# First layer's stick-breaking attention: the order of its steps, item by item, and one activation table set for Exp and Ln

## What is computed

```python
z = jnp.einsum('bqhd,bkhd->bhqk', q_blk, k).astype(jnp.float32) * scale
mask = key_pos[None, :] < q_pos[:, None]
log_1mb = jnp.where(mask, jax.nn.log_sigmoid(-z), 0.0)
after = lax.cumsum(log_1mb, axis=3, reverse=True) - log_1mb
w = jnp.where(mask, jnp.exp(jax.nn.log_sigmoid(z) + after), 0.0)
return jnp.einsum('bhqk,bkhd->bqhd', w.astype(v.dtype), v)
```

## Time and profile before

| | |
|---|---|
| median of 3 runs | 4190.07 us (4188.62 to 4195.27) |
| the profiled execution, its own time | 4190.46 us |
| its span, first to last instruction | 4188.7 us |
| TensorE clock granted, mean over the span | 0.917 of full |
| TensorE busy, share of the span (page) | 89% |
| the stretch of `Stick`, first sum matmul to last `XL` | 466.4 to 657.7 us |

### The profile page before, as it was taken

The page is one execution under the profiler, slowest core; times in us unless marked ns, Lnnn a source line. Parts: engine busy times, 40 slices in busy tenths (PEclk is TensorE's granted clock), DMA queues, the critical chain, the costliest instruction groups (busy, mean ns, idle before and its releaser), DMA issues. The chain is left out here.

```text
span 4188.7 us, 48251 instructions
## 1 busy us (share of the span) xinstructions
PE 3738.1 (89%) x18866; PEld 3037.5 (73%) x18866; DVE 2024.5 (48%) x3934; ACT 1698.1 (41%) x3132; POOL 108.0 (3%) x120
## 2 busy tenths in 40 slices
PE   6999678989995898999797999999879999998799
PEld 5888436768883777778675777777767687887686
DVE  3144323364334566676435355555545456555542
ACT  3222463264332333333225344444432555555430
POOL 0011120000000000000000000000000000000000
PEclk9999889989996787778899999999989999999799
DMA  3333303112222112111311111010122211110221
GB/s 124 116 129 105 126 0 121 36 56 96 102 77 75 43 44 61 41 41 44 154 51 41 40 30 30 27 31 26 34 103 76 71 36 36 36 36 16 85 101 41
DMA packets 219706, 265.62 MB, mean 63 GB/s; under 512 B 62684, under 2 KB 142676, under 8 KB 218456
## 3 DMA queue, kind: packets, MB, share of 16 engines
q1 hardware_dynamic: 219480, 262.53, 19.2%
HBM read 191.95 MB, written 70.52 MB: 63 GB/s over the span
## 5 line engine op out<-in xcount | busy, mean ns | idle before, releaser
L320 PE MATMUL bank<-wh,XH 128*128 128x512 f32 x1344 | 554.4, 412 | 40.8 <-DVE wl L304 21.1
L320 PE MATMUL bank<-wh,XL 128*128 128x512 f32 x1344 | 529.4, 394 | 0.0
L320 PE MATMUL bank<-wl,XH 128*128 128x512 f32 x1344 | 529.4, 394 | 0.0
L2394 PE MATMUL bank<-XH,wh 128*128 128x512 f32 x1040 | 428.5, 412 | 32.0 <-DVE wl L2383 19.7
L2394 PE MATMUL bank<-XH,wl 128*128 128x512 f32 x1040 | 412.9, 397 | 0.0
L2394 PE MATMUL bank<-XL,wh 128*128 128x512 f32 x1040 | 411.8, 396 | 0.0
L320 PEld LDWEIGHTS bank<-wh,XH 128*128 128x128 f32 x1344 | 256.3, 191 | 104.3 <-issue 39.2
L320 PEld LDWEIGHTS bank<-wh,XL 128*128 128x128 f32 x1344 | 256.5, 191 | 60.0 <-issue 10.0
L320 PEld LDWEIGHTS bank<-wl,XH 128*128 128x128 f32 x1344 | 255.7, 190 | 55.1
L320 PE MATMUL bank<-XH,wh 128*128 128x512 f32 x704 | 278.6, 396 | 5.7 <-DVE XL L1504 5.7
L304 DVE TENSOR_TENSOR wl<-raw,wh 128x1024 fp32r<-128x1024 f32 x128 | 157.0, 1241 | 255.0 <-ACT wh L295 253.4
(11 more groups left out here) (408 smaller groups left out, 7236.2 us busy)
## 6 DMA issues: line engine op xcount, KB each, us to landing
sc_zt<-stage SPq DMA_DIRECT2D x88, 256.0 KB, 2.0
raw<-in_att_w_in SPq DMA_DIRECT2D x33, 512.0 KB, 4.2
raw<-in_even_w_in SPq DMA_DIRECT2D x32, 512.0 KB, 5.0
raw<-in_odd_w_in SPq DMA_DIRECT2D x32, 512.0 KB, 4.4
raw<-in_rec_w_in SPq DMA_DIRECT2D x32, 512.0 KB, 4.0
sc_h<-H SPq DMA_DIRECT2D x24, 512.0 KB, 2.6
sc_z<-stage SPq DMA_DIRECT2D x40, 256.0 KB, 2.0
z<-sc_z SPq DMA_DIRECT2D x8, 1024.0 KB, 5.5
```

The source lines that it names most:

```text
L320: done = e.matmul(out, lhsT, rhs, start=k == 0 and j == 0, stop=k == NK - 1 and j == 2)
L2394: done = e.matmul(bank[:, :], x[:, k, :], y[:, k, ts], start=k == 0 and j == 0, stop=k == NK - 1 and j == 2)
```

## The change

`order` becomes a list of steps written out by `stick_order`. The 48 items stand in the same sequence as before (key blocks from the last to the first, the 4 heads inside), and each turn t of the list holds: `begin` of item t (z on PE; Abs, Exp and Ln on ACT; the softplus on DVE), `sum` of item t-2 (steps 4 and 5), `weigh` of item t-3 (step 6) and, for a key block 0, `mix` of item t-4 (step 7). `ve_kept` of head 0 to 3 stands in turns 12, 15, 18 and 21. On ACT, a set that holds both Exp and Ln is loaded once ahead of the list.

```diff
+def stick_order():
+
+    items = [(h, half, kb) for half in (1, 0) for kb in range(4 * half + 3, -1, -1) for h in range(4)]
+    order = []
+    for t in range(len(items) + 4):
+        for what, lag in (("begin", 0), ("sum", 2), ("weigh", 3)):
+            if 0 <= t - lag < len(items):
+                order.append((what, *items[t - lag]))
+        if t >= 4 and items[t - 4][2] == 0:
+            order.append(("mix", *items[t - 4]))
+        if t in (12, 15, 18, 21):
+            order.append(("kept", (t - 12) // 3, 0, 0))
+    return order
...
-        self.order = [(h, half, kb, part) for half in (1, 0) for kb in range(4 * half + 3, -1, -1)
-                      for part in range(3) for h in range(4)]
+        self.order = stick_order()
...
-            if part == 0:
+            if what == "begin":
...
                 e.matmul(bank[:, 0:n], self.k[h][:, kb * P:(kb + 1) * P], self.q[h][:, 512 * half + off:512 * (half + 1)],
                          start=True, stop=True).then_inc(*self.zed.up(h, half, kb))
-                if kb < top:
-                    self.pe_weighted(e, h, half, kb + 1)
-            elif part == 2:
+            elif what == "sum":
...
-            if kb == 0 and part == 2 and h == 3:
-                for g in range(4):
-                    self.pe_weighted(e, g, half, 0)
+            elif what == "weigh":
+                self.pe_weigh(e, h, half, kb)
...
+        e.preload_act_table_set("natural_log_exp_and_others")
...
                 e.activation(a[:, 0:n], a[:, 0:n], ACT.Exp, scale=-1.0).then_inc(*self.soft.up(h, half, kb))
-            elif part == 1:
                 e.wait_ge(*self.soft.at(h, half, kb))
                 e.activation(l[:, 0:n], a[:, 0:n], ACT.Ln, bias=1.0).then_inc(*self.logged.up(h, half, kb))
-            else:
+            elif what == "sum":
                 e.wait_ge(*self.sums.at(h, half, kb))
...
-                for g in range(4):
-                    e.wait_ge(*self.mixed.at(g, half))
-                    e.activation(c.XH[:, 4 + g, qc], self.g[g][:, qc], ACT.Copy).then_inc(*self.high.up(g, half))
+                e.wait_ge(*self.mixed.at(h, half))
+                e.activation(c.XH[:, 4 + h, qc], self.g[h][:, qc], ACT.Copy).then_inc(*self.high.up(h, half))
```

More of the change, by code:

```diff
@@ L99 @@
     tensor_copy = tensor_reduce = tensor_tensor_scan = reciprocal = bn_stats = bn_aggr = issue
-    copy_predicated = memset = dma_start = issue
+    copy_predicated = memset = dma_start = preload_act_table_set = issue
 class Turns:
@@ L1262, in ve_kept, with pe_weigh @@
         e.tensor_tensor(c.XL[:, h, :], self.kept[h][:, :], f32(c.XH[:, h, :]), ALU.subtract).then_inc(*self.kepl.up(h))
-    def pe_weighted(self, e, h, half, kb):
+    def pe_weigh(self, e, h, half, kb):
         off, n = self.width(half, kb)
@@ L1278, in pe @@
         e.wait_ge(*self.tables.at("after"))
-        for h, half, kb, part in self.order:
+        for what, h, half, kb in self.order:
             off, n = self.width(half, kb)
             bank, top = self.c.banks[h], 4 * half + 3
-            if part == 0:
+            if what == "begin":
                 if kb == top and half == 1:
@@ L1324, in ac @@
                 e.activation(w[:, 0:n], bank[:, 0:n], ACT.Exp).then_inc(*self.expd.up(h, half, kb))
-            if kb == 0 and part == 2 and h == 3:
+            elif what == "mix":
                 qc = slice(512 * half, 512 * (half + 1))
-                for g in range(4):
-                    e.wait_ge(*self.mixed.at(g, half))
-                    e.activation(c.XH[:, 4 + g, qc], self.g[g][:, qc], ACT.Copy).then_inc(*self.high.up(g, half))
+                e.wait_ge(*self.mixed.at(h, half))
+                e.activation(c.XH[:, 4 + h, qc], self.g[h][:, qc], ACT.Copy).then_inc(*self.high.up(h, half))
     def po(self, e, before):
@@ L1334, in po @@
             e.memset(self.r[h][:, :], 0.0).then_inc(*self.run.up(h, 1, 8))
-        for h, half, kb, part in self.order:
+        for what, h, half, kb in self.order:
             off, n = self.width(half, kb)
-            if part == 2 and kb:
+            if what == "sum" and kb:
                 e.wait_ge(*self.sums.at(h, half, kb))
@@ L1341, in po @@
                     .then_inc(*self.run.up(h, half, kb))
-            if half == 1 and kb == 0 and part == 2:
+            elif what == "sum" and half == 1:
                 e.wait_ge(*self.sums.at(h, 1, 0))
@@ L1352, in ve @@
         e.wait_ge(*self.tables.at("after"))
-        for h, half, kb, part in self.order:
+        for what, h, half, kb in self.order:
             off, n = self.width(half, kb)
             s, w = self.spl[h], self.w[h]
-            if part == 1:
+            if what == "begin":
                 e.wait_ge(*self.logged.at(h, half, kb))
@@ L1368, in ve @@
                 done.then_inc(*self.plus.up(h, half, kb))
-                if half == 1 and h == 3 and 2 <= kb <= 5:
-                    self.ve_kept(e, 5 - kb)
-            elif part == 2 and kb >= 4 * half:
+            elif what == "sum" and kb >= 4 * half:
                 e.wait_ge(*self.expd.at(h, half, kb))
                 e.tensor_tensor(w[:, 0:P], w[:, 0:P], self.after[:, :], ALU.mult).then_inc(*self.maskw.up(h, half, kb))
-            if kb == 0 and part == 2 and h == 3:
+            elif what == "kept":
+                self.ve_kept(e, h)
+            elif what == "mix":
                 qc = slice(512 * half, 512 * (half + 1))
[L1376 to L1383, removed]
+                gate = self.g[h][:, qc]
+                e.wait_ge(*self.weighted.at(h, half, 0))
+                e.wait_ge(*self.gates[h].at())
+                e.tensor_tensor(gate, c.banks[4 + h][:, :], gate, ALU.mult).then_inc(*self.mixed.up(h, half))
+                e.wait_ge(*self.high.at(h, half))
+                e.tensor_tensor(c.XL[:, 4 + h, qc], gate, f32(c.XH[:, 4 + h, qc]), ALU.subtract).then_inc(*self.low.up(h, half))
 VECS = {"mu": 0, "w0": 48, "a0": 56, "k_k": 64, "k_a": 72, "r_k": 80, "gain": 88, "bias": 96}
```

## The result

| | before | changed |
|---|---|---|
| median of the runs, us | 4192.67 (4 runs, 4188.62 to 4197.06) | 4131.59 (4 runs, 4127.65 to 4133.41) |
| the profiled execution, us | 4190.46 | 4131.08 |

The ratio is 0.9846, with a 95% interval of 0.9824 to 0.9868: faster, by 1.5%. The time forecast was 4132.

A forecast was written before the change was run, and what follows sets the result against it. No engine was full; a chain of waits set the time. Stage end 472.8 + 116.0 + 1 + 4 + 5.1 = 598.9 against 657.7, 58.8 us less, so 4190.46 becomes 4131.7; range 4122 to 4149.

The forecast's parts named there:

- PE's price: Attention matmuls: a unit, 128 columns of one fp32 matmul, costs 0.214 us at full clock; a wide turn 3.43 us.
- Start: First turns of the stage: PE's first sums at about 463.2 us, turn 8 at about 472.8, worst 474.
- Body and meeting of the halves: From turn 8: 542 units take 116.0 us, plus 1 for turns 8 to 11 and 4 where the halves meet.
- End: Last product and mixes: the stage ends 5.1 us behind PE's last matmul.
- Sum: Whole stage: ends at 598.9 against 657.7, 58.8 us less, so 4131.7 us for the program.
- C: Next stage is held by something with its own time, so the gain is waited away: 4190 us; chance 0.03.
- D: In-order queues make items go one at a time, each costing its whole chain: 66 us more, 4256; chance 0.03.
- E: PE at half clock throughout the body: 230 us in place of 116, program 4246 us; chance 0.02.
- B: PE's mean clock stays at 0.88 in the body: 15.8 us more than forecast, 4147.5; chance 0.14.
- F: Only the table loads' 30.8 us leave the chain, PE's waits otherwise stay: 4159.7 us; chance 0.04.
- The drain: ACT table switches: the skill adds some 1.38 us each, 63.8 for 24; the forecast went by 30.8 without it.

The follow-up runs named there:

- two runs on PE and ACT work: Changed kernel without the matmul on R in the 24 wide items: stage 124.76 us; changed kernel with an extra ACT pass in each: stage 140.71 us.
- later split: Changed kernel with XH and XL of half 1 moved from the mix to turns 43 to 46: stage 135.73 us, whole 4134.30 us.
- order only: Changed kernel without the preloaded table set, so the new order with the tables as before: stage 226.89 us, whole 4220.64 us, ratio to before 1.0062.
- set-only kernel: Kernel before, in its old order, with one table set holding Exp and Ln loaded once: stage 168.34 us, whole 4160.16 us, ratio 0.9912.
- more ACT work: Changed kernel with one more ACT pass of 512 columns behind the Ln of each wide item: stage 140.71 us, whole 4145.60 us (one run).

## Why the prediction was right

- *PE's price.* 0.214 us a unit held: 3.43 us for a wide turn, and 77.99 of 78 us busy at clock 1.00. The two runs on PE and ACT work show that PE is the bound there.
- *Start.* Turn 8 was forecast for 472.8 and began at 471.72. In this profile all was 1.09 us earlier before the stage began (q of the fourth head at 460.75 for 461.84), so the stepping was right within 0.1.
- *Body and meeting of the halves.* The second of these terms was mis-sized. From turn 8 to the end of PE's last matmul (595.13+1.13) it took 124.5 us, where 542 units need 116.2: 8.3 lost, 5 forecast. By stretch (z of turns 8, 32 and 40 at 471.72, 548.00 and 568.32; 354, 62 and 126 units) the losses are 0.4, 7.0 and 0.9 us. The forecast had 1 for turns 8 to 11, 4 for the meeting and nothing behind it. The mechanism was the forecast one (ACT and DVE exchanging the mix among narrow steps), but PE lost 7.0 us by it: 3.7 in the two waits, about 2.5 in 5 us at half clock, the rest in small steps. I had taken 4 with an upper end of 8, "the lag plus some slow clock behind it", and that end was the nearer one. The later split took 4.6 of it away.
- *End.* Forecast 5.1 us from PE's last matmul to the last XL, measured 4.8 (596.26 to 601.03).
- *Sum.* The stage was to lose 58.8 and lost 55.6. The profiled execution lost 59.4: 1.1 came ahead of the stage and 2.7 behind it, where nothing was changed and where profiles of the same code differ by 10 and more. So the whole agreed better than the stage did (4131.59 for 4132), and that part is luck: the stage alone would have given 3.2 us more. The forecast also took 8.4 us as what a measurement can tell from no change; the intervals in the table are 9 to 18 us wide to either side.
- *The rivals.* C (nothing moves) fell with the stage's end, D (lock step) and E (half clock) with the wide turns. B, the clock, was a small part of the truth in one place of 5 us. F, the loads alone, is now measured: 27.6 us of 55.6. It was nearly the loads' 30.8 us, but not for its reason: one of the two loads of a round was hidden, and 10.6 us of slow clock behind the gaps made up for most of it.
- *The drain.* The Trainium skill ("ScalarE: Activation LUTs", section "What ACT_TABLE_LOAD costs") adds some 1.38 us of drain to a switch. With order only, two loads and four passes fit into 5.00 us; 2 x 1.28 + 4 x 0.61 is 5.0. The trace doesn't agree: no drain of that size shows. The set-only kernel puts a load on the chain at 1.42 us, so the forecast's 1.28 was 0.14 short.

What the forecast did not say is how much the two halves of the change depend on each other: the set gave 27.6 us in the old order and 86.6 in the new one (226.89 to 140.32), and the order cost 31.0 with the old tables and gave 28.0 with the new set (168.34 to 140.32).

## What to carry to other kernels

Grouping heads by function saved table loads here but made every round end in a serial hand-over; interleaving the items hid the hand-over only when the tables didn't have to change, so the two are to be decided together. Read a change of 10 us from its stage and not from the whole when a stage elsewhere spreads by as much. When a pipeline is made even for its wide turns, price the turns where the widths change apart: there the work is too short to hide an exchange between two engines that a wide turn hides.

## What was not expected of the hardware

- The length of a wait alone doesn't tell whether PE's clock falls behind it. With 1.30 us of waiting in every 5.00, the stretch from 500 to 600 us of the order-only kernel shows 0.99; from 610 to 640, among its narrow turns with waits of 0.3 to 3.15 us, it shows 0.60. In the set-only kernel the wide rounds with 1.73 us of waiting in every 15.7 had no slow matmul, but a wait of 2.03 us between narrower rounds had some behind it (the sum matmul at 600.33 starts 1.17 us after the one at 599.16, where 0.64 is the step at full clock). In the kernel before, the clock fell after 3.16 us and stayed at 1.00 over the round behind a wait of 3.34 us, which ended at 611.63. In the changed one it fell after 1.63 and 2.08 us close behind each other, with narrow matmuls between. In this order:

```profile
500.00:600.00 100.00, 73.87 (x164) 29.11 (x162) 28.70 (x40) 98.20 (x121) 24.68 (x21) 0.99 0.00 0
610.00:640.00 30.00, 18.63 (x56) 13.28 (x54) 9.57 (x24) 27.46 (x44) 3.84 (x7) 0.60 0.00 1
```

```profile
599.16 1.38 PE L1296 MATMUL bank<-sp,ntri 128*128 128x384 f32 x2 [2.03 <-DVE sp L1368]
600.33 1.49 PE L1298 MATMUL bank<-R,nones 128*128 128x384 f32 x2
```

```profile
611.63:623.11 11.48, 8.03 (x32) 6.02 (x32) 4.67 (x13) 9.72 (x19) 2.97 (x4) 1.00 0.00 0
```

- The recurrence of the second layer, the same code in all kernels, took from 710.5 us (order only) to 723.7 (more ACT work) from the first to the last start of a matmul or weight load that reads its tile `bet`, at a mean clock of 0.76 to 0.78 where I looked. Why it differs from run to run was not looked into.
